# The experts' second pass: who subtracts a slot's rounded part, GpSimd or VectorE

## The reference

```
a   = gelu(einsum("ced,cd->ce", u_emb[idx], hx))     # first pass: each token with its experts' u rows
out = einsum("ce,ced->cd", gate * a, v_emb[idx])     # second pass: the gated sum of its experts' v rows
```

## Time and profile before

| | before |
|---|---|
| median of 3 runs | 3267.0 us (3264.32 to 3268.2) |
| the profiled execution, device time | 3261.49 us |
| its span in the trace | 3259.7 us |
| TensorE busy | 3122.5 us, 96% |
| VectorE busy | 2252.7 us, 69% |
| GpSimd busy | 1271.7 us, 39% |
| slot_lo on GpSimd (L200), whole kernel | x362, 902.6 us, mean 2495 ns |
| slot_lo on VectorE (L200), whole kernel | x198, 242.8 us, mean 1226 ns |
| the multiply (L1417) | x128, 226.3 us, mean 1769 ns |

### The profile page before, as it was taken

One profiled execution on the slowest core, in us unless ns is written; L12 is line 12 of the kernel. 1 busy time (PEld: TensorE's weight loads), 2 busy tenths in 40 slices (PEclk: granted clock), 3 DMA queues, 4 the chain that ended last, 5 costly groups with the idle time before them and its releaser, 6 DMA issues.

```text
span 3259.7 us, 42914 instructions
## 1 busy us (share of the span) xinstructions
PE 3122.5 (96%) x16170; PEld 2700.5 (83%) x16170; DVE 2252.7 (69%) x3332; ACT 1217.1 (37%) x1818; POOL 1271.7 (39%) x635
## 2 busy tenths in 40 slices
PE   7999999998999998999999999999999999999998
PEld 5877778998989898988888978888588888888886
DVE  7899868998888885998998863204487666522105
ACT  3334543233333333333333353323436564333225
POOL 0010144552344444888888634442020001444432
PEclk9999999999999999999999999999999999999999
DMA  3211133444899999888898722223122222322222
GB/s 126 94 61 46 59 123 123 134 133 155 293 323 338 330 333 345 308 322 318 310 325 314 262 91 97 97 96 126 59 85 72 78 78 78 120 100 97 97 91 91
DMA packets 172859, 548.15 MB, mean 168 GB/s; under 512 B 16825, under 2 KB 41913, under 8 KB 172529
## 3 DMA queue, kind: packets, MB, share of 16 engines
q1 hardware_dynamic: 107968, 380.10, 33.3%
q0 software_dynamic: 36864, 134.23, 12.2%
q10 hardware_dynamic: 27824, 31.08, 2.7%
HBM read 490.60 MB, written 54.55 MB: 167 GB/s over the span
## 4 chain that ended last, share of the span: by engine, by line
PE 61%; DVE 19%; DVEq 9%; DMA 4%; issue 2%; ACTq 2%; ACT 2%; POOL 1%; SPq 0%; POOLq 0%
PE ps L212 41%; PE ps L1111 7%; PE ps L1506 6%; DVEq L1432 4%; DMA experts_back<-experts_dram 3%; DVE conv_out L760 2%; ACTq L1187 2%; DVE gated_lo L1425 1%; DMA ring<-in_stream 1%; PE ps L1086 1%; DVEq L747 1%; ACT slot_parts L196 1%; DVE slot_parts L200 1%; PE ps L1785 1%; DVE h_rows L1439 1%
## 5 line engine op out<-in xcount | busy, mean ns | idle before, releaser
L200 POOL TENSOR_TENSOR slot_parts<-ring,slot_parts 128x1024 fp32r<-128x1024 f32 x362 | 902.6, 2495 | 1332.8 <-ACT slot_parts L196 1332.2
L212 PE MATMUL ps<-h_norm_hi,slot_parts 128*128 128x512 f32 (+1 forms) x4576 | 1361.5, 374 | 54.0 <-DVE slot_parts L200 41.9
L212 PEld LDWEIGHTS ps<-h_norm_hi,slot_parts 128*128 128x128 f32 x4576 | 851.9, 189 | 172.6 <-DVE slot_parts L200 46.2
L212 PE MATMUL ps<-x_low,slot_parts 128*128 128x512 f32 (+1 forms) x2224 | 813.0, 366 | 0.0
L196 ACT ACTIVATE slot_parts<-ring 128x1024 fp32r<-128x1024 f32 x560 | 589.7, 1053 | 484.5 <-DMA ring<-in_stream 315.6
L1111 PE MATMUL ps<-gated_hi,slot_parts 128*128 128x384 f32 x2048 | 549.0, 339 | 36.4 <-DVE gated_lo L1425 24.6
L200 DVE TENSOR_TENSOR slot_parts<-ring,slot_parts 128x1024 fp32r<-128x1024 f32 x198 | 242.8, 1226 | 345.4 <-ACT slot_parts L196 345.1
L212 PEld LDWEIGHTS ps<-x_low,slot_parts 128*128 128x128 f32 x2224 | 422.1, 190 | 49.0
L1111 PEld LDWEIGHTS ps<-gated_hi,slot_parts 128*128 128x128 f32 x2048 | 371.9, 188 | 70.1 <-issue 52.9
L1111 PE MATMUL ps<-gated_lo,slot_parts 128*128 128x384 f32 x1024 | 342.9, 335 | 0.0
L1417 DVE TENSOR_TENSOR gated<-gates_back,experts_back 128x384 f32<-128x384 f32 x128 | 226.3, 1769 | 57.3 <-DMA experts_back<-experts_dram 50.6
(11 more groups left out here) (434 smaller groups left out, 4075.2 us busy)
## 6 DMA issues: line engine op xcount, KB each, us to landing
ring<-in_stream SPq DMA_DIRECT2D x560, 512.0 KB, 3.5
experts_dram<-experts SPq DMA_DIRECT2D x64, 384.0 KB, 5.8
gates_dram<-gates_by_key ACTq DMA_DIRECT2D x24, 1024.0 KB, 18.5
gates_back<-gates_dram SPq DMA_DIRECT2D x32, 768.0 KB, 6.0
experts_back<-experts_dram SPq DMA_DIRECT2D x64, 384.0 KB, 6.0
x_res<-in_xT SPq DMA_DIRECT2D x4, 512.0 KB, 8.2
x_res<-in_xT SPq DMA_DIRECT2D x1, 2048.0 KB, 8.3
v_row<-in_stream,pick_table POOLq DMA_INDIRECT x128, 6.9
```

Source lines behind the costliest of these rows:

```text
L200: e.tensor_tensor(to[:, BUFFER[n], 1, :], ring[:, n % RING, :], to[:, BUFFER[n], 0, :].bitcast(F32), ALU.subtract).then_inc(s_lo, 1)
L212: mm = e.matmul(psum, w2[wv][:, k, :], x2[xv], start=start and v == 0, stop=stop and v == 2)
```

## The change

GpSimd no longer subtracts in this pass: its queue holds only the gathers, all 128 in a row, each still behind its buffer's wait. VectorE makes slot_lo of every slot, as the next instruction behind gated_lo of the same slot and ahead of the step's row sums. The two separate ones at the end go. Nothing else changes: what is computed, the buffers and the other engines' orders stay.

```diff
         for b in range(2):
             e.wait_ge(w_out[b], 64 * ((BLOCKS + 1 - b) // 2))
-        for s in range(ROWS_V):
+        for s in range(STEPS):
             v_row(s)
-        e.wait_ge(s_lo, ORDINAL[n_v])
-        for n in range(n_v, n_v + NKEY - 2):
-            slot_lo(e, n)
-            for s in sums_after(n - n_v - 1):
-                if s + ROWS_V < STEPS:
-                    v_row(s + ROWS_V)
         leave(e)
...
                 e.wait_ge(v_hi, i + 1)
                 e.tensor_tensor(G_lo[:, i % GBUF, :], GV[:, i % GBUF, :], G_hi[:, i % GBUF, :].bitcast(F32),
                                 ALU.subtract).then_inc(v_lo, 1)
+                slot_lo(e, n_v + i)
                 if j == 2:
...
-                if i >= NKEY - 2:
-                    e.wait_ge(s_lo, ORDINAL[n_v + i])
-                    slot_lo(e, n_v + i)
         leave(e)
```

## The result

| | before | after |
|---|---|---|
| median of 17 runs each | 3268.2 us (3256.8 to 3278.6) | 3284.9 us (3256.6 to 3304.1) |
| ratio, with its 95% interval | | 1.0051 [1.0026, 1.0075] |
| profiled execution, span | 3261.5, 3259.7 us | 3277.0, 3275.2 us |
| the second pass, first to last matmul of L1111 | 1285.4 to 1885.0, 599.6 us | 1290.6 to 1899.6, 609.0 us |

The forecast was 3239 with a range of 3217 to 3262. Of the 15.5 us between the two spans, 9.4 lie in the second pass, 0.9 behind it, and 5.2 ahead of it, where the program is the same; in the other traces of this case the second pass begins anywhere from 1278 to 1295 us, so I take the 5.2 for scatter and explain the 9.4. The medians are 16.7 us apart, with an interval of 8.5 to 24.5; how much of that lies in the pass, one trace of each kernel cannot tell.

A forecast was written before the change was run, and what follows sets the result against it. VectorE, held up by GpSimd's subtraction, was taken to set the second pass's pace. 111 slots x (4.72 - 4.47) = 28 us off the 3259.7 span gives 3232, or 3239 us as the runs' median; range 3217 to 3262.

The forecast's parts named there:

- the lock: Second pass: VectorE's multiply is shut out by GpSimd's subtraction, costing about 2.2 us a slot, which the change gives back.
- Rival 3: The long multiply isn't GpSimd's doing, so VectorE's slot becomes 5.67 us: 105 us slower, 3372; chance 0.05.
- Rival 4: VectorE leaves GpSimd few openings and the six gather buffers run dry; at 32 us per gather, 3388 us; chance 0.01.
- what is late next: slot_lo stands behind a multiply that waits for experts_back; TensorE can start at the landing plus 2.35 us.
- The limit of 5.55 us: Longest experts_back landing behind gates_back that leaves TensorE unheld; 5.97 us without gates_back ahead.
- That costs 0.95 and, for the spread, some 0.15 more: 1.1 us in four slots.: TensorE's wait for late experts_back, taking landings of 6.5 us behind gates_back and 5.6 without; pace 4.44 us a slot.
- the sign of being wrong from 7 us on: The prediction called itself wrong if experts_back lands at 7 us median.
- 0.03 us a slot: Allowance for landings lengthened by denser traffic, against relief from later gathers; brings the pace to 4.47 us.
- it undoes itself: Argument against rival 2: at pace 4.7 the traffic is what it was before, when the median landing was 6.1 us.
- Rival 2: Landings lengthen some 0.8 us with denser traffic, pace 4.7: 0 to 10 us won; chance 0.17 including what lies between.
- a cost that I don't have: A lower granted clock in the second pass, where it stayed at 1.00 before; no size was given.
- no floor: Rival 1, the floor: TensorE or transfers set the pace, 4.16 to 4.36 a slot, 40 to 62 us won; chance 0.15.

The follow-up runs named there:

- e8: The kernel before, GpSimd still subtracting, with gated_lo of slot j-1 put ahead of VectorE's multiply of slot j: 3259.9 us, ratio 0.9978 to the kernel before.
- e1: The kernel after with slot_lo of slot j-1 put ahead of VectorE's multiply of slot j: 3239.0 us, ratio 0.9925 to the kernel before.
- e2: The kernel after with gated_lo and slot_lo of slot j-1 both ahead of the multiply of slot j: 3219.8 us, ratio 0.9866 to the kernel before.
- e4: The kernel after with only the first six gathers, row sums rereading them (wrong sums, timing only): 3202.5 us, ratio 0.9815 to the kernel before.
- e10: The kernel after with gates_back issued three slots earlier, where no experts_back goes out: 3240.2 us, ratio 0.9918 to the kernel before.
- e11: e2 with 14 deliberate stalls of TensorE, waiting for slot_lo of the slot two ahead: 3325.4 us, ratio 1.0173 to the kernel before.
- e12: e2 and e10 together: 3206.1 us, ratio 0.9808 to the kernel before.

## Why the prediction was wrong

**Right: the lock.** "One shut out by the other" holds: the multiply's median went from 2.75 to 0.55 when GpSimd stopped subtracting, and stayed at 2.76 in e8, where only the order changed; VectorE's slot is 3.5, and the gaps of 1.25 every eleventh slot are gone. Rival 3 is out. Rival 4 too: the gathers were issued in 1.11 us on the mean, and VectorE waited for no row.

**Right: what is late next.** The way from experts_back over multiply, gated_lo and slot_lo takes 2.30 us in the chain after (2.35 forecast), and e1 and e2 confirm it by taking it apart. The limit of 5.55 us is right to the digit: in all 28 pairs behind gates_back TensorE's wait is the landing less 5.55 us, or nothing, to within 0.05 us.

**The step that failed: "That costs 0.95 and, for the spread, some 0.15 more: 1.1 us in four slots."** I put one number for each kind of pair, 6.5 and 5.6, against a limit and took the difference, with 0.15 for the spread. But a wait past a limit is paid landing by landing and nothing comes back for the early ones. Taken so, the landings of the kernel before already give 1.16 + 0.16 = 1.3, and those after give 1.74 + 0.06 = 1.8 us in four slots, 50 us over the stretch instead of 30. The median over all landings, which I named as the sign of being wrong from 7 us on, was 5.6 and hid it.

I named denser traffic and allowed 0.03 us a slot for it, with the new moment of the gather as a relief. Over both kinds of pair the mean landing did stay at 6.1, as "it undoes itself" had it; but behind gates_back it rose from 6.7 to 7.2, and fell only where there was room to spare. Rival 2 was this mechanism, priced at 0 to 10 us won; its break-even needed only the excess to double.

Why the landings behind gates_back grew later and more uneven stays open. It is not that one stall makes the next: the 13 landings that follow a stall of over 1.8 us take 6.8 us on the mean, the 14 that follow a shorter one or none 7.5, and e2, almost without stalls, still has 7.1. What e4, e8 and e10 show is that it takes gates_back just ahead and the gathers, and that the gathers' moment matters.

**The term that was missing: the clock.** The last line of the prediction calls a lower granted clock "a cost that I don't have"; so it stood at nothing. In the stretch, of 13 stalls of over 1.8 us, ten had a spell at 1.2 GHz that began in them or within 1 us behind them, and none came elsewhere. Two slots that hold a spell of 3.4 us take up to 10.17 us instead of 8.6; over the ten, one of them double, the rows come to 16 us. Stalls of up to 1.7 us brought none, neither here nor in the kernel before.

e11 shows for stalls of 4.7 us and more that it is the stall: the same kernel as e2 with stalls put in has 14 spells where e2 has one. For the shorter ones it rests on the count. In the second passes of all twelve traces there are 60 such spells, each begun in a stall of over 1.8 us or within 1.5 us behind one; 19 more such stalls, none over 3.4 us, had no spell. What decides among those, no run here settles. It is not the profiled execution alone: over the whole span the granted clock was 0.977 to 0.986 in the 17 executions of the kernel after, and 0.986 to 0.993 in the 48 of the kernel before that were timed beside the experiments.

The sum, from slot 9 to 120: 111 x 4.16 = 462 us; landings past the limit 50; clock 16; the rest, 5, is of the size of what the starts behind 22 waits cost (two slots behind a wait take 8.6 us, not 8.3): 533, which is the stretch. The forecast had 462 + 30 + 3. The 37 to 38 between them turn 28 won into 9 lost. Without the clock the change would have won some 7 us; that is an estimate from these rows, as no run has the stalls without the spells.

**The traffic** was no floor: 346 and 352 GB/s in e2 and e12, above the 340 that I took as the most the trace had shown, and near the 357 that busy share and rate gave.

Of the Trainium skill's "SBUF — State Buffer", the section on the DVE blocking DMA and the bandwidth-pool intuition behind it: its factor of five, 620 to 3100 ns, is for a `tensor_copy` on VectorE, and the stretch has none. No run here shows a gather starved, though 3.5 us of each slot were VectorE's. A gather's issue took 1.11 us on the mean in the kernel after; in e1 the median was 1.68, and still no row sum waited for its row.

## What to carry to other kernels

When work moves onto an engine that runs in order, ask first what it will stand behind: here the same move cost 17 us with slot_lo behind a multiply that waits for a transfer, and won 24 with it in front. Price a wait past a limit by the single landings, not by their median, and look what TensorE's granted clock does in and behind the stalls. And where two transfers go out together and only one is urgent, send the large one a step earlier, at a step in which nothing else leaves.

## What the runs showed of the hardware that I had not expected

- A VectorE operation with two SBUF inputs (128x384, 0.55 us alone) beside a GpSimd subtraction took 2.75, ending 0.42 us behind GpSimd's; without that GpSimd work, 256 of 256 took 0.55 to 0.56.
- TensorE's granted clock fell to 0.50 for 3.4 us (once 6.8) in or within 1 us behind ten of thirteen stalls of 1.8 to 4.7 us, and for 6.8 to 10.2 us in all fourteen of 4.7 to 7.4 us, where the fall began 2.7 us into the stall whose rows stand above. For stalls up to 1.7 us, in the kernels before and after, it did not fall.
- A transfer of 384 KB landed in 3.1 us on the mean with the gathers gone and nothing just ahead, in 4.8 with the gathers gone and 768 KB ahead, in 4.9 with the gathers and nothing just ahead, and in 7.2 (at most 10.3) with both. With both, but the gathers at another moment (e8), it was 5.4.
